# A block-product up projection and a four-pass down projection in a two-layer transformer kernel on one Trainium2 core

## The reference

```python
D_MODEL = 1024; SEQ = 1024; D_FF = 2816; CONV_WIDTH = 3

def conv_ffn(h, w_up, conv_w, conv_b, w_down):
    gu = h @ w_up                                   # 1024 x 5632
    gate, up = gu[..., :D_FF], gu[..., D_FF:]
    gate = causal_conv(gate, conv_w) + conv_b       # three taps along the tokens, per feature
    return (jax.nn.gelu(gate, approximate=False) * up) @ w_down

    x = x + merged @ w_out[l]
    x = x + conv_ffn(rmsnorm(x, ffn_norm_g[l]), w_up[l], conv_w[l], conv_b[l], w_down[l])
```

## Time and profile before

| | |
|---|---|
| time, median of 3 runs | 2604.42 us (2604.04 to 2605.08) |
| span of the profiled execution | 2600.4 us |
| what lies around the span, against the median | 4.0 us |
| PE busy | 2518.6 us (97%) |
| DVE busy | 1399.9 us (54%) |
| ACT busy | 705.5 us (27%) |
| POOL busy | 671.5 us (26%) |
| moved by DMA | 158.21 MB |

### The profile page before, as it was taken

The page is one execution under the profiler, slowest core; times in us unless marked ns, Lnnn a source line. Parts: engine busy times, 40 slices in busy tenths (PEclk is TensorE's granted clock), DMA queues, the critical chain, the costliest instruction groups (busy, mean ns, idle before and its releaser), DMA issues.

```text
span 2600.4 us, 32782 instructions
## 1 busy us (share of the span) xinstructions
PE 2518.6 (97%) x12324; PEld 2078.4 (80%) x12324; DVE 1399.9 (54%) x1812; ACT 705.5 (27%) x1005; POOL 671.5 (26%) x368
## 2 busy tenths in 40 slices
PE   8999999999999999999999979999999999999998
PEld 5777787877788888888888858888888887788886
DVE  7847656725635551455135673367767764633454
ACT  4232222223212110011001232155566661222121
POOL 3223332322332333333333322300100002222221
PEclk9999999999999999999999989999999999999999
DMA  4133342413231111111121111100000001111112
GB/s 178 49 114 130 114 162 97 146 49 127 85 96 50 48 48 49 49 48 48 48 65 48 57 43 41 49 17 9 11 13 8 9 9 59 33 41 32 33 47 73
DMA packets 45835, 158.21 MB, mean 61 GB/s; under 512 B 5524, under 2 KB 6804, under 8 KB 45626
## 3 DMA queue, kind: packets, MB, share of 16 engines
q1 hardware_dynamic: 40900, 139.34, 17.0%
q10 hardware_dynamic: 4854, 17.74, 2.0%
HBM read 146.03 MB, written 13.39 MB: 61 GB/s over the span
## 4 chain that ended last, share of the span: by engine, by line
PE 86%; DVE 9%; issue 2%; ACT 1%; DMA 1%; POOL 0%; DVEq 0%; SPq 0%; ACTq 0%; POOLq 0%
PE PS L569 66%; PE PS L1045 3%; PE PS L978 3%; PE PS L984 2%; PE PS L1017 2%; PE PS L727 1%; PE PS L762 1%; DVE cols L2350 1%; PE PS L968 1%; PE PS L610 1%; PE PS L602 1%; DVE SC L2018 1%; PE PS L1195 1%; PE PS L1211 1%; PE PS L1055 1%
## 5 line engine op out<-in xcount | busy, mean ns | idle before, releaser
L569 PE MATMUL PS<-H,w_hl 128*128 128x512 f32 x6624 | 1548.1, 393 | 29.2 <-DVE H L1833 9.0
L569 PEld LDWEIGHTS PS<-H,w_hl 128*128 128x128 f32 x6624 | 1242.3, 189 | 311.1 <-issue 32.8
L544 POOL CAST w_hl<-w_raw 128x1024 fp32r<-128x1024 f32 x180 | 201.6, 1120 | 1871.1 <-PE PS L569 1480.8
L546 POOL TENSOR_TENSOR w_hl<-w_raw,w_hl 128x1024 fp32r<-128x1024 f32 x180 | 460.1, 2556 | 14.4
L569 PE MATMUL PS<-FF,w_hl 128*128 128x512 f32 x1056 | 239.8, 389 | 0.0
L569 PEld LDWEIGHTS PS<-FF,w_hl 128*128 128x128 f32 x1056 | 198.3, 188 | 41.1
L978 PE MATMUL PS<-CKV,QN 128*128 128x512 f32 (+1 forms) x576 | 141.9, 364 | 0.0
L1528 ACT ACTIVATE SC<-SC,vec 128x1024 f32<-128x1024 f32 x22 | 25.4, 1153 | 392.5 <-DVE SC L2216 392.4
L1045 PE MATMUL PS<-PT,CKT 128*128 128x256 f32 x960 | 120.7, 283 | 1.5 <-DVE PT L2366 1.5
L1045 PEld LDWEIGHTS PS<-PT,CKT 128*128 128x128 f32 x960 | 117.8, 191 | 2.4 <-DVE PT L2366 1.7
L2366 DVE TENSOR_TENSOR PT<-PS,PT 128x512 fp32r<-128x512 f32 (+1 forms) x192 | 103.6, 596 | 22.9 <-ACT PT L1624 22.4
(11 more groups left out here) (313 smaller groups left out, 2357.0 us busy)
## 6 DMA issues: line engine op xcount, KB each, us to landing
w_raw<-in_units SPq DMA_DIRECT2D x182, 512.0 KB, 3.6
AW<-in_ada SPq DMA_DIRECT2D x48, 512.0 KB, 4.4
X<-in_x SPq DMA_DIRECT2D x8, 512.0 KB, 8.5
SC<-in_x ACTq DMA_DIRECT2D x8, 512.0 KB, 3.6
out<-X SPq DMA_DIRECT2D x16, 256.0 KB, 2.1
m_part<-GTA ACTq DMA_DIRECT2D x7, 512.0 KB, 3.2
M<-m_part SPq DMA_DIRECT2D x7, 512.0 KB, 6.7
g_part<-GTB ACTq DMA_DIRECT2D x6, 512.0 KB, 2.8
```

What stands on the lines that cost most here:

```text
L544: pool.tensor_copy(hi_part, raw).then_inc(w_hi, 1)
L546: pool.tensor_tensor(lo_part, raw, hi_part.bitcast(F32), ALU.subtract).then_inc(w_split, 1)
L569: mm = pe.matmul(PS[:, out_at + a:out_at + a + m], w(s, wp, w0 + k), src[:, o:o + m], start=(k == 0 and wp == 0 and xp == 0), stop=(k == k ...
```

## The change

The up projection of a gate/up pair is done as a product of 2x2 blocks with seven block products in place of eight (Strassen's scheme, in Winograd's form with sums reused). The weights of a pair are cut into gate and up, and into input features 0 to 511 and 512 to 1023; the activations are cut into the two halves of the features and the two halves of the tokens. The seven activation operands (`B11`, `BT1`, `B21`, `B22`, `BT2`, `BT4`, `BT3`) are made once, around the end of `out1`. The weight sums are made by DVE for every pair from the raw weights (`weight_sums`), and POOL splits the seven operands of each pair into seven slots (`WS`). A product is 4 blocks x 3 matmuls of 128x512. Products share PSUM banks: ACT copies partial results out (`snap`), and later products add onto them in place.

All 22 pairs come first. Their results no longer fit in SBUF, so 20 of the 22 chunks are written to DRAM (`ff_spill`), and x goes to DRAM as well and comes back (`x_reload`). The down projection then runs in four passes of 4, 6, 6 and 6 chunks (`DOWN`). The first pass takes weights for two outputs from one unit. There are two raw buffers for a pair's weights (`w_raw`, `w_raw2`). The loads of x for `out1` move from ACT's queue to SP's.

```diff
-FF_PASSES = [8, 8, 6]
+DOWN = [[0, 1, 20, 21], [2, 3, 4, 5, 6, 7], [8, 9, 10, 11, 12, 13], [14, 15, 16, 17, 18, 19]]
+KEPT = 2
+PRODUCTS = 7
+HK = KC // 2
...
+    OPERANDS = [B11, BT1, B21, B22, BT2, BT4, BT3]
+    BANKS = [0, 1, 2, 1, 0, 3, 0]
+    OPENS = [True, True, True, False, False, True, False]
+    ADDENDS = [[a11, SUM1, a12, SUM4, SUM2, a22, a21] for a11, a12, a21, a22 in BLOCKS]
...
 @block.sync
+        for p in range(2, FFC):
+            sp.wait_ge(w_split, u0 + 2 * p - 2)
+            load_pair(p)
+            ff_spill(p - 2)
...
 @block.gpsimd
+        def operand(p, n, q):
+            hi_part, lo_part = WS[n][:, 0:HK * P], WS[n][:, HK * P:2 * HK * P]
...
+            pool.tensor_copy(hi_part, ADDENDS[q][n][:, :]).then_inc(w_hi, 1)
+            pool.wait_ge(w_hi, p * PRODUCTS + (up0 + n + 1))
+            pool.tensor_tensor(lo_part, ADDENDS[q][n][:, :], hi_part.bitcast(F32), ALU.subtract).then_inc(w_st, 1)
...
+        def later_operands(p, q):
+            for n in range(PRODUCTS):
+                pool.wait_ge(st_prod, p * PRODUCTS + (n + 1 - PRODUCTS))
+                operand(p, n, q)
...
 @block.tensor
+        def up_pair(p, q, first=False):
+            at0 = 2048 * q
+            pe.wait_ge(st_free, p * 3 + 3)
+            for n in range(PRODUCTS):
+                pe.wait_ge(w_st, p * PRODUCTS + (n + 1))
+                if n == 3:
+                    pe.wait_ge(st_snap, p * 4 + 2)
+                elif n == 6:
+                    pe.wait_ge(st_snap, p * 4 + 3)
+                bank = at0 + 512 * BANKS[n]
+                for k in range(HK):
+                    for wp, xp in PASSES:
+                        mm = pe.matmul(PS[:, bank:bank + HALF], WS[n][:, (wp * HK + k) * P:(wp * HK + k + 1) * P],
+                                       OPERANDS[n][:, (xp * HK + k) * HALF:(xp * HK + k + 1) * HALF],
+                                       start=OPENS[n] and k == 0 and wp == 0 and xp == 0, stop=k == HK - 1 and wp == 1,
+                                       skip_group_check=True)
+                mm.then_inc(st_prod, 1)
+                if first and n == 1:
+                    norm_sum(before("norm2", "norm"), before("norm2", 2), early=before("norm2", "square") - 1)
+                elif first and n == 3:
+                    norm_spread(before("norm2", "norm"), before("norm2", 3))
...
+        def first_down():
+            pe.wait_ge(st_free, 6 + 3 * (FFC - 1))
+            for i in range(KC // 2):
+                for p in range(2):
+                    take(p, i + b("down0", p))
+                pe.wait_ge(w_split, u0 + i + 1)
...
 @block.scalar
+        def snap(p, n, dst, bank):
+            act.wait_ge(st_prod, p * PRODUCTS + n)
+            act.activation(dst, PS[:, bank:bank + HALF], ACT.Copy).then_inc(st_snap, 1)
+        def up_first(p, q):
+            snap(p, 1, GATE[:, 0:HALF], 2048 * q)
+        def up_rest(p, q, kept=None):
+            snap(p, 2, KEEP[q][:, HALF:T], 2048 * q + 512)
...
+            snap(p, 5, GATE[:, HALF:T], 2048 * q)
+            snap(p, 6, KEEP[q][:, 0:HALF], 2048 * q + 1536)
+            act.wait_ge(cv_ready, p + 1)
+            act.activation(PROD, CONV, ACT.Gelu, bias=vec[:, bass.ds(p + VEC["conv_b"], 1)]).then_inc(gl_ready, 1)
+            act.wait_ge(xt, p + xts[0] + 1)
+            act.activation(dst[:, 0:T], PROD, ACT.Copy).then_inc(hi, 1)
+        def slot_free(p):
+            act.wait_ge(ff_out, p * 16 - 16)
...
 @block.vector
+        def weight_sums(p, q, names):
+            a11, a12, a21, a22 = BLOCKS[q]
...
+                    v.tensor_tensor(SUM1[:, :], a21, a22, ALU.add).then_inc(st_sum, 1)
...
+                    v.tensor_tensor(a21, a11, a21, ALU.subtract).then_inc(st_sum, 1)
...
+                    v.tensor_tensor(SUM2[:, :], SUM1[:, :], a11, ALU.subtract).then_inc(st_sum, 1)
...
+                    v.tensor_tensor(SUM4[:, :], a12, SUM2[:, :], ALU.subtract).then_inc(st_sum, 1)
...
+        def up_pair(p, q, sums=True, kept=None):
+            v.wait_ge(st_prod, p * PRODUCTS + 3)
+            v.wait_ge(st_snap, p * 4 + 1)
+            chain(v.tensor_tensor(GATE[:, 0:HALF], PS[:, at0 + 1024:at0 + 1536], GATE[:, 0:HALF], ALU.add))
+            v.sem_inc(st_free, 1)
+            if sums:
+                weight_sums(p + 1, 1 - q, (1, 3, 2, 4))
+            v.wait_ge(st_snap, p * 4 + 3)
+            chain(v.tensor_tensor(GATE[:, HALF:T], PS[:, at0 + 512:at0 + 1024], GATE[:, HALF:T], ALU.add))
+            v.sem_inc(st_free, 1)
+            chain(v.tensor_tensor(GATE, GATE, R2, ALU.mult))
+            chain(v.tensor_scalar(CONV, SC[:, 0:T], tap(0), None, ALU.mult))
...
+            v.wait_ge(st_prod, p * PRODUCTS + 7)
+            chain(v.tensor_tensor(GATE.rearrange("p (a c) -> p a c", a=2),
+                                  PS[:, at0:at0 + HALF].unsqueeze(1).to_broadcast([P, 2, HALF]),
+                                  KEEP[q][:, :].rearrange("p (a c) -> p a c", a=2), ALU.add))
+            v.sem_inc(st_free, 1)
+            v.wait_ge(gl_ready, p + 1)
+            chain(v.tensor_tensor(PROD, PROD, R2, ALU.mult))
+            v.tensor_tensor(PROD, PROD, GATE, ALU.mult).then_inc(xt, 1)
...
+            v.tensor_tensor(dst[:, T:2 * T], PROD, dst[:, 0:T].bitcast(F32), ALU.subtract).then_inc(lo, 1)
```

More of the change, by code:

```diff
@@ new lines, in _ @@
+        number = u0 + 2 * FFC
+        last = PRODUCTS * (FFC - 1)
+        d0 = before("down0", "unit")
+        sp.wait_ge(x_out, 16 * KC)
+        x_reload(0)
+        sp.wait_ge(w_split, d0 - 2)
+        for s in range(2):
+            sp.wait_ge(w_in[s], 16 * (d0 // 2))
+        for s in range(2):
+            sp.dma_start(w_raw[:, s * UW:(s + 1) * UW], t_in["units"][d0 + s]).then_inc(w_in[s], 16)
+        number += 2
+        sp.wait_ge(st_prod, last + 2)
+        ff_load(0, 0)
+        ff_load(0, 1)
@@ new lines, in _, with plain_units @@
+        down0 = before("down0", "unit")
+        more = PRODUCTS * FFC - 2 * FFC
+        def plain_units(first, last, his, used):
+            with pool.Fori(first // 2, last // 2) as i:
+                for s in range(2):
+                    pool.wait_ge(w_used, 2 * i + (s - 1 - used))
+                    hi_part, lo_part, raw = split_unit(s, 16 * i + 16)
+                    pool.sem_inc(w_seen, 1)
+                    pool.tensor_copy(hi_part, raw).then_inc(w_hi, 1)
+                    pool.wait_ge(w_hi, 2 * i + (s + 1 + his))
+                    pool.tensor_tensor(lo_part, raw, hi_part.bitcast(F32), ALU.subtract).then_inc(w_split, 1)
@@ new lines, in later_down, with turn @@
+        def later_down(n):
+            phase = f"down{n}"
+            u0 = before(phase, "unit")
+            last = n == len(DOWN) - 1
+            def turn(i, s, split=False):
+                take(2 + s, i + b(phase, 2 + s))
+                pe.wait_ge(w_split, i * 2 + u0 + s + 1)
+                for a in (0, HALF) if split else (None,):
+                    down_unit(n, (u0 + s) % 2, (2 + s) * 1024, opens=not a, n_cols=T if a is None else a + HALF,
+                              a0=a or 0, fresh=not s).then_inc(done[2 + s], 1)
+            turns = KC // 2 - last
+            with pe.Fori(0, turns) as i:
+                for s in range(2):
+                    turn(i, s)
+            if last:
+                turn(turns, 0)
+                turn(turns, 1, split=True)
@@ L1483, in attn_residual, with operand_hi @@
[L1483 to L1489, removed]
-                one(last, 1, half, HALF)
+            def operand_hi(dst, k, src):
+                act.activation(dst[:, k * HALF:(k + 1) * HALF], src, ACT.Copy, scale=v1("ffn_g", k + (HK if dst is B21 or dst is B22 else 0))
+                               ).then_inc(hi, 1)
@@ new lines, in _ @@
+        up_pair(0, 0)
+        up_pair(1, 1)
+        with v.Fori(1, FFC // 2 - 1) as i:
+            chain.enter(i - 1, 2 * 7)
+            for q in range(2):
+                up_pair(i * 2 + q, q)
+            chain.leave(FFC // 2 - 2)
+        up_pair(FFC - 2, 0, kept=0)
+        up_pair(FFC - 1, 1, sums=False, kept=1)
+        xts[0] += FFC
+        his[0] += FFC
+        residual("down0", 0, squares=(), landed=True)
+        for q in range(2):
+            chain(v.tensor_tensor(modb[:, 16 * q:16 * q + 16], modb[:, 16 * q:16 * q + 16],
+                                  vec[:, VEC["b_both"]:VEC["b_both"] + 16], ALU.add))
```

535 lines of the change are left out of this document (375 added, 160 removed).

## The result

Before 2604.75 us (2604.04 to 2606.38), after 2620.66 us (2619.35 to 2624.13): ratio 1.0062, 95% interval 1.0048 to 1.0076. The change costs 15.9 us; I had said 2614, with 2580 to 2645 as the range. The profiled span went from 2600.4 to 2622.3 us, 21.9 more; that is over the 15.9 of the medians, since the profiled execution of the kernel after was its slowest (2624.13 us) and that of the kernel before lies 2.5 under its median. Of the 21.9, 3.75 lie ahead of the up stage: the output projection ends at 800.96 where before it ended at 797.21, and the windows show a granted clock of 0.98 between 200 and 400 us, where the change has no edit. The up and down stages together went from 721.7 to 738.8 us, +17.1, and 1.0 lies behind them.

What follows compares the result with a forecast made beforehand. The up projection was taken as bound by PE's number of matmuls. Terms -59.8, +53.2, +11.2 and +5.0 gave +9.6 on the 2600.4 us span, plus 4.0 around it: 2614 us, range 2580 to 2645.

Steps and rivals of the forecast that it cites:

- Matmuls saved, -59.8: Up stage: 84 matmuls a pair for 96, -59.8 us over 22 pairs; PE alone would need 19.04 us a pair.
- Prices: Up stage: estimated instruction times, such as 0.61 us for POOL's half-width cast and 1.30 for its subtraction.
- DVE and POOL exclude each other: Up stage: SBUF instructions of DVE and POOL exclude each other, 4.5 us of DVE waits, 21.7 us a pair.
- The floor of 20.6: Up stage: DVE's 9.3 us and POOL's 11.3 us of held port add to at least 20.6 us a pair.
- The ring: Up stage: dependency loop through ACT's in-order queue, DVE and the fourth and fifth products, 19.3 us a pair without collisions.
- Pairs 2 to 21, +53.2: Up stage from the third pair on: 20 pairs at 21.7 us against PE's 19.04, +53.2 us.
- First two pairs: Start of up stage: late DVE and ACT work makes pair 0 take 26.4 us and pair 1 26.6, +11.2 us.
- The sum: Whole kernel: -59.8 + 53.2 + 11.2 + 5.0 = +9.6 us, giving 2614 us.
- Down, three stops, +5.0: First down pass: PE waits three times for DVE's add of the second PSUM region, 1.65 us each, +5.0 us.
- The clock rival: Up stage: PE's clock falls after the stall in each pair, 2631 to 2648 us; chance 0.15.
- The port hides, 19.3: Up stage: POOL works while DVE waits, leaving only the ring at 19.3 us a pair, 2562 us; chance 0.12.
- A queue is late: Up stage: SP waits for spills before weights or reloads, so PE stops for raw weights, 2635 us; chance 0.06.

Runs made afterwards that it cites:

- the last run: Kernel after with high parts and first conv tap on ACT, ACT's second PSUM copy before its high copy, late second PSUM regions, two sums early: 2559.00 us.
- four edits together: Kernel after with ACT's second PSUM copy before its high copy, high parts on ACT, second PSUM regions taken late in up stage and first down pass: 2593.33 us.
- orders alone: Kernel after with ACT's second PSUM copy before its high copy, DVE's first two sums earlier, second PSUM regions taken late; all engines keep their work: 2612.20 us.
- the two edits together: Kernel after with ACT's second PSUM copy before its high copy and DVE's four sums cut to 64 columns from pair 1 on: 2593.76 us, ratio 0.9965.

## Why the prediction was right, and where it was off

- *Matmuls saved, -59.8, PE alone 19.04.* Right; the last run reaches 19.07.
- *Prices.* POOL 0.61 and 1.29 for 0.61 and 1.30.
- *DVE and POOL exclude each other, 4.5 us of waits on DVE, 21.7 a pair.* Right in size (the listed waits add to 4.6). The eleven means less their own durations are 0.05, 0, 0.41, 0.98 (sums), 0.55, 0.37, 0.55, 0.38, 0.01, 0.74 and 0.37: 4.4. They fall in other places than I had laid them. DVE is 83% busy, not over 85%, and PE stands 1.8 us a pair before the fourth product, not 2.7. The row that the prediction calls DVE's add at 1138.14 is the multiply with R2; the reading, that an instruction with a tile in PSUM keeps its time, holds. The Trainium skill (SBUF — State Buffer, section "SBUF: two separate sides") says that the port is held for whole instructions. The trace agrees: a sum of 64 columns, 0.22 us alone, took 1.30 behind a subtraction.
- *The floor of 20.6 with an unused rest.* In no order tried did the pair go under 21.69 with all work left in place. 20.6 itself was not reached, so that it is the floor stays an estimate; one of the two engines is at work for all but 0.3 us of the pair, so the 1.1 between lie in the passing from one instruction to the next.
- *The ring, 19.3.* Too long by 0.7. With narrow POOL work, where DVE waits 1.25 us a pair for the copy of the fifth product, the pair is 19.44 with 0.86 of collisions in the ring; with casts on ACT and a high clock 21.8 with 3.3. Both leave 18.5 to 18.6. In the changed kernel the ring then takes 18.6 + 2.6 = 21.2, and with falls of 1.5 behind 7 of 20 stops 21.7: as long as DVE's queue by chance. I had weighed it only without its collisions, as a chain that the port makes irrelevant.
- *Pairs 2 to 21, +53.2.* 860.93 to 1295.08 is 434.2 us, 20 x 21.71; forecast 434.
- *First two pairs, 53.0 from the end of the output projection.* This is the term that was too small: 60.0, and 57.8 in the run with the late down region, whose up stage is the same. PE starts 5.45 late, and pairs 0 and 1 then take 25.8 and 28.8, with a stop of 6.97 before pair 1's fourth product, behind pair 0's late chain. The prediction gave PE's wait for the second PSUM region nothing, and let pair 0 end 26.4 behind the projection. It ends at 31.2, and with that region taken late it ends at 31.2 (four edits together) and 30.0 (orders alone), where the unchanged start reached 30.0 too in the run with the late down region. So the take is where the lateness shows, not what makes it: apart from gaps under 0.3, DVE idles only 1.40, 1.40 and 1.13 us between 799.53 and 826.73, and PE, if it starts early, waits for DVE and POOL later. Pair 1 is a matter of ACT's order: with the copy order alone it takes 23.1. That DVE's queue sets the end of pair 0 is argued from these rows; which part of it I had too short no run tells.
- *The sum.* For the stage the terms give 731.4 us (53.0, 434 and 244.4) and the profile 738.8 (60.0, 434.2 and 244.7): +7.4, nearly all of it in the first two pairs. The medians miss by 6.3. That the long pairs came out to 0.2 us in 434 is partly luck: the ring, which I had too long, came to the same length as DVE's queue by chance.
- *Down, three stops, +5.0.* 4.4, and lost time: without them the down passes take 4.8 less. Spills, reloads and raw weights: no stop, as forecast.
- *The clock rival.* The falls came, behind seven of 20 stops, and cost nothing by themselves, since DVE's queue takes the same 21.7 at a clock of 1.00. With the casts on ACT, filling the hole gave 20 us back. The Trainium skill (TensorE: Matmul & The Clock Gate, section "HAM oscillation") warns of just such a loop. The run with the casts on ACT agrees, with a fall in 14 of 19 pairs; in the changed kernel it is 7 of 20, at no cost.
- *The port hides, 19.3*: refuted by the trace after. *A queue is late*: not seen.

What stays open: why the same stop of 2.45 us lowered the clock in some pairs and not in others, whether an order exists that brings the pair nearer to 20.6, and what in DVE's queue makes pair 0 end 4.8 us later than forecast. No run told these.

## What to carry over

Where two engines share a port, add their held times as one queue, and compare that with the bound of the engine that the change relieves: seven products for eight saved 2.72 us a pair, and the operands put 20.6 us on a port with room for 19.04. If a removed cost moves nothing, look for a second chain of the same length before calling it hidden; only the two edits together moved it. Here moving work off the port and reordering pay only together: orders alone left the pair at 21.69, casts moved without the new copy order cost 29 us, and both with the late takes gained 27. And a stop that is removed is not yet time gained: look whether the work behind it ends earlier.

## What the runs showed of the hardware that was not expected

- A DVE instruction behind POOL pays for POOL's instruction, not for its own width: 64 columns (0.22 us alone) took 1.30 (DVE's timeline of the run with copy order and narrow sums). Narrower is not cheaper there; fewer is.
- DVE's multiply with one SBUF input (0.75) is stretched like the two-input ones, to 1.55; ACT's copies and casts kept 0.58 to 0.64 beside both engines.
- With the casts on ACT the same stop of 2.45 us was followed by twelve matmuls of 3.03 us in 5 of 19 pairs and of 4.2 to 4.6 in the others.
